# Inverse roots taken on ScalarE, squares summed on VectorE, and a first round that reaches into its third weight unit

## The reference, cut to what matters

```python
def _rmsnorm(x, g):
    y = x * rsqrt(mean(x * x, axis=-1) + 1e-6)
    return y * g

def _swiglu(h, w_in, w_out):
    gate, up = split(h @ w_in, 2)
    return (silu(gate) * up) @ w_out

for i in range(4):                       # g = norm_gains[i]
    h = h + 0.5 * _rmsnorm(_swiglu(_rmsnorm(h, g[0, 0]), ...), g[0, 1])
    h = h +       _rmsnorm(mixer(_rmsnorm(h, g[1, 0])),        g[1, 1])
    h = h + 0.5 * _rmsnorm(_swiglu(_rmsnorm(h, g[2, 0]), ...), g[2, 1])
```

## Time and profile before

| | us |
|---|---|
| three runs, median | 2501.04 |
| profiled execution, its own time | 2503.98 |
| its span | 2502.2 |
| PE busy | 2379.8 (95% of the span) |
| POOL busy | 1813.3 (72%) |
| DVE busy | 1481.2 (59%) |
| ACT busy | 1011.8 (40%) |
| granted TensorE clock, mean | 0.976 of 2.4 GHz |

### The profile page before, as it was taken

One profiled execution on the slowest core, in us unless ns is written; L12 is line 12 of the kernel. 1 busy time (PEld: TensorE's weight loads), 2 busy tenths in 40 slices (PEclk: granted clock), 3 DMA queues, 4 the chain that ended last, 5 costly groups with the idle time before them and its releaser, 6 DMA issues.

```text
span 2502.2 us, 53983 instructions
## 1 busy us (share of the span) xinstructions
PE 2379.8 (95%) x20898; PEld 2295.7 (92%) x20898; DVE 1481.2 (59%) x1830; ACT 1011.8 (40%) x1497; POOL 1813.3 (72%) x853
## 2 busy tenths in 40 slices
PE   6999999999999799999999788999999999999997
PEld 6999989999999789999999578988999999988997
DVE  5872137845862336863882868536882783234982
ACT  4344344344343434344443453324343434444342
POOL 5887827887887507886888696746888788746886
PEclk9999999999999989999999789999999999999999
DMA  5564614563564304563555132013555455433553
GB/s 168 175 195 129 180 61 135 171 206 118 170 194 127 119 19 141 168 200 119 173 183 170 70 113 83 4 37 95 175 183 169 143 178 192 135 109 101 174 188 109
DMA packets 89951, 348.87 MB, mean 139 GB/s; under 512 B 9968, under 2 KB 11760, under 8 KB 89712
## 3 DMA queue, kind: packets, MB, share of 16 engines
q1 hardware_dynamic: 89840, 347.31, 44.2%
HBM read 346.22 MB, written 1.05 MB: 139 GB/s over the span
## 4 chain that ended last, share of the span: by engine, by line
PE 83%; DVE 6%; POOL 4%; issue 3%; ACT 3%; DMA 0%; DVEq 0%; SPq 0%; ACTq 0%; POOLq 0%
PE bank L295 22%; PE bank L297 22%; PE bank L296 22%; PE bank L625 3%; POOL w_lo L1261 2%; PE bank L393 2%; PE bank L357 2%; PE bank L358 2%; PE bank L359 2%; PE bank L338 2%; POOL x_lo L1287 1%; DVE hid_hi L1475 1%; DVE hid L1473 1%; ACT w_hi L882 1%; PE bank L535 1%
## 5 line engine op out<-in xcount | busy, mean ns | idle before, releaser
L1261 POOL TENSOR_TENSOR w_lo<-raw,w_hi 128x1024 fp32r<-128x1024 f32 (+2 forms) x608 | 1604.1, 2663 | 594.6 <-ACT w_hi L882 572.3
L295 PE MATMUL bank<-x_hi,w_hi 128*128 128x272 f32 (+1 forms) x3380 | 991.7, 293 | 39.5 <-POOL x_lo L1287 16.3
L297 PE MATMUL bank<-x_hi,w_lo 128*128 128x272 f32 (+1 forms) x3380 | 981.8, 290 | 0.0
L296 PE MATMUL bank<-x_lo,w_hi 128*128 128x272 f32 (+1 forms) x3380 | 978.4, 289 | 0.0
L882 ACT ACTIVATE w_hi<-raw 128x1024 fp32r<-128x1024 f32 (+2 forms) x608 | 660.3, 1115 | 257.2 <-PE bank L297 204.5
L295 PEld LDWEIGHTS bank<-x_hi,w_hi 128*128 128x128 f32 x3380 | 643.6, 190 | 52.5 <-issue 30.4
L296 PEld LDWEIGHTS bank<-x_lo,w_hi 128*128 128x128 f32 x3380 | 645.3, 191 | 0.3
L297 PEld LDWEIGHTS bank<-x_hi,w_lo 128*128 128x128 f32 x3380 | 644.2, 191 | 0.0
L1477 DVE TENSOR_TENSOR hid_lo<-hid,hid_hi 128x272 f32 (+3 forms) x176 | 423.1, 2404 | 20.2
L295 PE MATMUL bank<-hid_hi,w_hi 128*128 128x272 f32 (+1 forms) x1408 | 404.9, 288 | 0.9 <-POOL w_lo L1261 0.8
L297 PE MATMUL bank<-hid_hi,w_lo 128*128 128x272 f32 (+1 forms) x1408 | 403.5, 287 | 0.0
(11 more groups left out here) (278 smaller groups left out, 2457.5 us busy)
## 6 DMA issues: line engine op xcount, KB each, us to landing
raw<-in_ffn_in SPq DMA_DIRECT2D x352, 512.0 KB, 3.6
raw<-in_ffn_out SPq DMA_DIRECT2D x128, 704.0 KB, 4.1
raw<-in_sb_in SPq DMA_DIRECT2D x48, 512.0 KB, 3.6
raw<-in_rw_in SPq DMA_DIRECT2D x24, 512.0 KB, 3.3
raw<-in_sb_out SPq DMA_DIRECT2D x16, 512.0 KB, 3.6
raw<-in_mla_out SPq DMA_DIRECT2D x8, 512.0 KB, 3.2
raw<-in_rw_lora SPq DMA_DIRECT2D x8, 512.0 KB, 4.7
raw<-in_rw_out SPq DMA_DIRECT2D x8, 512.0 KB, 3.2
```

What stands on the lines that cost most here:

```text
L295: nc.tensor.matmul(o, wh, xh[:, k, cols()], start=start, stop=False)
L296: nc.tensor.matmul(o, wh, xl[:, k, cols()], start=False, stop=False)
L297: last = nc.tensor.matmul(o, wl, xh[:, k, cols()], start=False, stop=stop)
L1261: nc.gpsimd.tensor_tensor(w_lo[:, s, w], raw[:, s, w], w_hi[:, s, w], ALU.subtract).then_inc(lo_ready, 1)
```

## The change

Three edits and what hangs on them.

1. The root and the reciprocal become a logarithm and an exponential on ACT, `exp(-0.5*ln(mean+eps))`, for every RMS norm, for `kk` and for the head norm. The result of the output norm is written straight to bank 4. Both functions are in one table set, which takes the place of the Sqrt table and of those loaded around the attentions; ACT has 21 table loads in place of 27. At the very first norm two loads are put in, one ahead of each of the two.
2. The squares of the eight tiles are added by DVE in three steps (4 tiles, 2, 1), and PE has one matmul by ones in place of eight. FILL goes from 25 to 17.
3. `first_round` runs units 0 and 1 with each tile and, where a norm stands ahead of it, a block of unit 2 with each odd tile; then the four blocks of unit 2 that are left, and all of unit 3. The sum stands behind the sixth of these twelve. In time mixing unit 2 comes whole and then unit 3.

```diff
-FILL = 25
+SUM_AFTER = 6
+FILL = 17
@@ PE
-            def input_sum(k, cut=None):
+            def input_sum(cut=None):
...
-                pe.wait_ge(hsq_ready, n["hsum"])
-                last = nc.tensor.matmul(bank[5][:, cut:L], ones, m[:, k, cut:L], start=k == 0, stop=k == DT_ - 1)
+                pe.wait_ge(hacc_ready, n["hsum"])
+                nc.tensor.matmul(bank[5][:, cut:L], ones, acc[:, cut:L], start=True, stop=True).then_inc(hsum_done, 1)
@@ first_round
+                paced, early = [], DT_ // 2 if behind_norm else 0
+                for k in range(DT_):
+                    paced += [(0, k), (1, k)] + ([(2, k // 2)] if early and k % 2 else [])
+                rest = [(2, k) for k in range(early, DT_)] + [(3, k) for k in range(DT_)]
+                for at, (s, k) in enumerate(paced + rest):
+                    if at == len(paced) + SUM_AFTER and behind_norm:
+                        input_sum(sum_cut)
+                    if k == 0:
+                        pe.wait_ge(lo_ready, sec.start + s + 1)
+                        pe.wait_ge(bank_free[s], uses[s] + 1)
+                    if s == 0:
+                        pe.wait_ge(x_ready, base + k + 1)
@@ latent attention
-                    if s == 0 and k or (s, k) in ((1, 6), (1, 7), (1, 0)):
-                        input_sum((k - 1) % DT_)
+                    if (s, k) == (3, 2):
+                        input_sum()
@@ ACT
-            def root(b, width, doubled=False):
-                nc.scalar.activation(std[:, cols()], bank[b][:, cols()], ACT.Sqrt, ...).then_inc(std_ready, 1)
+            def inverse_root(dst, b, width, doubled=False):
+                n["log"] += 1
+                nc.scalar.activation(std[:, cols()], bank[b][:, cols()], ACT.Ln, ...).then_inc(log_ready, 1)
+                act.wait_ge(log_ready, n["log"])
+                nc.scalar.activation(dst[:, cols()], std[:, cols()], ACT.Exp, scale=-0.5).then_inc(rstd_ready, 1)
...
-                nc.scalar.preload_act_table(ACT.Sqrt)
+                nc.scalar.preload_act_table_set("natural_log_exp_and_others")
...
                 def kk_roots():
-                    nc.scalar.preload_act_table(ACT.Sqrt)
                     act.wait_ge(kkmax_ready, 1)
-                    nc.scalar.activation(ex[:, :, :], ex[:, :, :], ACT.Sqrt, scale=64.0).then_inc(kkroot_ready, 1)
+                    nc.scalar.activation(ex[:, :, :], ex[:, :, :], ACT.Ln, scale=64.0).then_inc(kklog_ready, 1)
+                    act.wait_ge(kklog_ready, 1)
+                    nc.scalar.activation(ex[:, :, :], ex[:, :, :], ACT.Exp, scale=-0.5).then_inc(kkroot_ready, 1)
@@ DVE
             def input_norm():
-                inverse_root(xr)
+                n["hsq"] += DT_
+                dve.wait_ge(hsq_ready, n["hsq"])
+                steps.link(nc.vector.tensor_tensor(m[:, 0:4, cols()], m[:, 0:4, cols()], m[:, 4:8, cols()], ALU.add))
+                steps.link(nc.vector.tensor_tensor(m[:, 0:2, cols()], m[:, 0:2, cols()], m[:, 2:4, cols()], ALU.add))
+                nc.vector.tensor_tensor(acc[:, cols()], m[:, 0, cols()], m[:, 1, cols()], ALU.add).then_inc(hacc_ready, 1)
+                inverse_root()
...
-                steps.link(nc.vector.reciprocal(ex[:, :, :], ex[:, :, :]))
```

More of the change, by code:

```diff
@@ L346, in first_round @@
                 n["x"] += DT_
[L347 to L349 removed]
+                paced, early = [], DT_ // 2 if behind_norm else 0
[6 more added lines that the diff above has]
+                    if k == 0:
                         pe.wait_ge(lo_ready, sec.start + s + 1)
                         pe.wait_ge(bank_free[s], uses[s] + 1)
[L352 to L363 removed]
+                    if s == 0:
+                        pe.wait_ge(x_ready, base + k + 1)
+                    o, wh, wl = bank[s][:, cols()], w_hi[:, s, P * k:P * k + P], w_lo[:, s, P * k:P * k + P]
+                    nc.tensor.matmul(o, wh, x_hi[:, k, cols()], start=(k == 0), stop=False)
+                    nc.tensor.matmul(o, wh, x_lo[:, k, cols()], start=False, stop=False)
+                    last = nc.tensor.matmul(o, wl, x_hi[:, k, cols()], start=False, stop=(k == DT_ - 1))
+                    if k == DT_ - 1:
+                        last.then_inc(unit_used, 1)
             def whole(s, j):
@@ L871, in _ @@
         def _(act):
-            n = dict(sq=0, sg=0, norm=0, xf=0, h=0, hid=0, head=0, mhead=0, vt=0, hsum=0, kept=0, cut=0)
+            n = dict(sq=0, sg=0, norm=0, xf=0, h=0, hid=0, head=0, mhead=0, vt=0, hsum=0, log=0, kept=0, cut=0)
             cols = lambda: slice(n["cut"], L)
@@ L904, in finish_norm @@
                 act.wait_ge(sq_free, 2 + squares - n["kept"])
-                root(b, width)
+                inverse_root(rstd, b, width)
                 if not parts:
@@ L930, in gained @@
                     split_hi(secs[0], 0, 3, first=True)
-                    for k in range(DT_):
-                        nc.scalar.activation(m[:, k, cols()], h[:, k, cols()], ACT.Square).then_inc(hsq_ready, 1)
+                    nc.scalar.activation(m[:, :, cols()], h[:, :, cols()], ACT.Square).then_inc(hsq_ready, DT_)
             def input_root():
@@ L936, in input_root @@
                 act.wait_ge(hsum_done, n["hsum"])
-                root(5, D)
+                inverse_root(xr, 5, D)
             def norm_out(half):
@@ L942, in norm_out @@
                 n["kept"] += 1
-                root(4, D, half)
+                inverse_root(bank[4], 4, D, half)
             def squares_of(sec):
@@ L1071, in latent_attention @@
                 take_tiles(s_ukv, 4, lambda t: mk[:, t, :] if t < NH else mv[:, t - NH, :], every=1)
-                nc.scalar.preload_act_table(ACT.Exp)
                 take_values(mvt)
@@ L1215, in head_roots @@
                     act.wait_ge(var_done, 4 * half + 4)
-                    nc.scalar.activation(ystd[0:8, half, :], bank[4 * half][0:8, 0:L], ACT.Sqrt, bias=ln_eps_col[0:8, :]).then_inc(bank_free[4 * half], 1)
+                    nc.scalar.activation(ystd[0:8, half, :], bank[4 * half][0:8, 0:L], ACT.Ln, bias=ln_eps_col[0:8, :]).then_inc(bank_free[4 * half], 1)
+                    act.wait_ge(bank_free[4 * half], uses_at["ln"][4 * half] + 3)
+                    nc.scalar.activation(yrs[0:8, half, :], ystd[0:8, half, :], ACT.Exp, scale=-0.5).then_inc(yrs_ready, 1)
                 def high_part(k):
@@ L1394, in _, with inverse_root @@
             take = iter(secs)
-            def inverse_root(dst=rstd):
+            def inverse_root():
                 n["std"] += 1
-                dve.wait_ge(std_ready, n["std"])
-                steps.link(nc.vector.reciprocal(dst[:, cols()], std[:, cols()]))
+                dve.wait_ge(rstd_ready, n["std"])
             def low_part(layer, sub, k):
@@ L1448, in last_product @@
                 n["kept"] += 1
-                inverse_root(bank[4])
+                b = 2 if two else 3
+                dve.wait_ge(bank_free[b], uses_at[sec.name_key][b] + sec.iters + 1)
+                inverse_root()
                 for k in range(DT_):
@@ L1791, in head_norm @@
                     scaled(k)
-                inverse_roots(0)
                 for k in range(4, 8):
```

39 lines of the change are left out of this document (7 added, 32 removed).

## The result

Four runs of the changed kernel took 2463.29 to 2470.09 us, median 2467.36; four of the kernel before on the same chip 2500.37 to 2503.74, median 2500.72. The ratio is 0.9863, with a 95% interval from 0.9846 to 0.9880: faster by 33 us. The forecast was 2459, with a range from 2445 to 2481. The profiled execution took 2467.77 us itself, its span is 2466.0, its mean clock 0.977 (before 0.976).

The account below looks back on a forecast made before the run. PE's matmuls were 83% of the span, but a POOL-DVE-ACT loop set each SwiGLU's end. Terms 14.7+5.0+7.3+3.2+2.6+7.8+1.4=42.0 us off 2503.98 gave 2462.0, in medians 2459, range 2445 to 2481.

Parts of the forecast that it names:

- Output norm: At each boundary: reciprocal replaced by an exponential, factor ready 1.36 us earlier, only 0.47 us come through behind POOL's fourth split.
- First round: Round behind a boundary, X being the last `x_lo`'s end: ends at X+6.5, 3.65 us sooner; third addition starts X+2.0, split X+2.1.
- SwiGLUs and last norm: Seven SwiGLUs: root-to-POOL-run falls from 7.16 to 6.2 us, run starts 2.1 us sooner, 14.7 in all; last norm 1.4.
- The very first round: The eighth SwiGLU in-section, at the kernel's start: POOL's run starts at 36.3 against 41.3, gaining 5.0 us.
- Stick-breaking layers: Both PE-bound in their projections: 2x3.65=7.3 us, plus 0.94 twice for the table load ahead of the attention.
- rival A: At all ten boundaries but latent attention's, the third addition starts behind the split; about 11 us, 2470; chance 0.28.
- Latent attention: Entry gated by DVE moves 1.3 us earlier, reciprocals of `rstd` give 1.3; sum 2.6, plus 1.28 for the table load.
- Time mixing: Boundary 0.5 us, `rstd` 1.35, and 6 (bounds 2 to 10) for the reciprocal over `kk` leaving DVE; sum 7.8.
- B: SwiGLUs: the loop finds a shorter rhythm or was misjudged, PE's gain comes through; 7x1.6 us more, 2448; chance 0.10.
- C: `first_round`, ten times: with 8 fillers fewer PE idles and its clock falls; 6 us each, 2519; chance 0.03.
- D: At 26 norms Ln and Exp each need a table load: two of 1.28 us each, 67 us cost; given nothing.
- short waits for `w_lo` in every SwiGLU round: Sign of the forecast in PE, with POOL's runs of four still 12.17 us apart; under B there are none.

Follow-up runs that it names:

- e4: The kernel before with the first edit alone (logarithm and exponential for every root, with the table loads): 2489.35 us, ratio 0.9971.
- e2: As e1, with PE's sum of squares behind the third of the last twelve blocks in place of the sixth: 2464.61 us, ratio 0.9870.
- e6: As e5, with PE's sum of squares behind the third of the last twelve blocks: 2442.66 us, ratio 0.9783.
- e12: The kernel before, unchanged, in one more profiled execution: one run, 2498.68 us.
- e1: The changed kernel, but POOL waits for DVE's third addition before splitting the fifth unit, at every boundary with a sum: 2462.27 us, ratio 0.9863.
- e10: As e6, with filling matmuls (8, 2 and 5) in PE's three waits at the end of latent attention: 2443.02 us, ratio 0.9772.
- e11: The kernel before with nothing changed but `up` and `hid` in PSUM: 2491.05 us, ratio 0.9963.
- e8: As e1, but for `kk` DVE takes the reciprocal over 2176 columns again: 2460.88 us, ratio 0.9854.
- e7: The kernel before with the second edit alone (DVE's three additions, one sum on PE, FILL 17), `first_round` waiting for each weight unit by itself: 2491.99 us, ratio 0.9975.
- e3: As e1, with the third edit undone in the eight SwiGLUs and the two stick-breaking layers: 2462.23 us, ratio 0.9866.
- e9: As e6, with the third edit undone in the SwiGLUs and stick-breaking layers, the sum behind the fourth of sixteen blocks: 2451.49 us, ratio 0.9806.
- e5: As e1, with DVE writing `up` and `hid` in the SwiGLUs to spare banks of PSUM in place of SBUF: 2448.47 us, ratio 0.9810.

## Why the prediction was right, and where it was not

The forecast of 2459 was 8.4 us below the median, and the range held it. The sum was 5.8 us too large (42.0 against 36.2 between the two spans), and some of its reasons were wrong. Latent attention fell 6.3 short; the other differences nearly cancel.

- **Output norm**: right. The additions stand straight behind the fourth split, which is what let 0.47 us through; the pair on ACT took 0.91 where 0.97 was reckoned.
- **First round**: right in its times, X+2.00, X+2.13, X+4.39 and X+10.44 against X+2.0, 2.1, 4.3 and 10.5.
- **SwiGLUs and last norm**: 15.6 forecast (14.7 and 1.4, less the 0.5 counted with the very first round), 16.7 measured over seven sub-layers. The step that failed is "the reciprocal leaves ... 6.2 us", with "an earlier end needs an earlier first run of POOL" read as an earlier root. The root's chain is only one of two. In the kernel before, `hid` had taken 0.78 us, and I had booked 0.4 of it as a split that it would no longer meet, without asking when the splits themselves would end. e4 shows that the reciprocals alone give these sub-layers nothing, e2 that an earlier root gives none either, e6 that it does as soon as `hid` waits for no split. The gain of 2.2 is 1.7 from POOL's run, which starts 18.68 us behind the additions in place of 20.36, and 0.5 from the next output norm. The 1.7 stands because edit 1 moved one chain and edit 2 the other, to within 0.06 us of each other (15.37 and 15.31 behind the additions). The prediction had worked out only one of them, so that its number came true here was luck.
- **The very first round**: 5.5 forecast with the output norm behind it, 5.0 measured (5.4 against e12).
- **Stick-breaking layers**: about 9.2 for both with their table loads, 8.1 measured. In the second, rival A happened and took 1.1 (e1 gives 1.3 back). In the first, 1.3 of its 5.6 is where the lower clock fell in the one execution (e12); 4.3 is left of 4.6.
- **Latent attention**: 3.9 forecast, 2.5 lost. The entry's additions met two splits (I had worked out the race for units of eight blocks, and here they have six and come up sooner); the earlier `rstd` met POOL's run, which ate its 1.3; and PE stood at the lower clock for some 14 us at the end in place of 7, which cost up to 3.5. e10 shows the clock's share to hang on three waits of PE. The unchanged kernel took 155.5 in e12 and 157.8 in e11, and the versions with POOL's wait 155 to 158 (e10 aside), so that a gain of the size forecast is not shown here.
- **Time mixing**: 7.8 forecast, 8.9 measured; against the mean of the three unchanged executions it is 7.3. The place was right: the wait of 3.48 us in `v` with the lower clock behind it is gone, as the prediction had said, and PE reaches L625 some 3 us sooner. Its credit to the reciprocal over `kk` was not: put back into the changed kernel, it costs nothing (e8), and the waits unit by unit alone do as much as edit 1 alone (e7, e4). The rest of the gain is spread over the sub-layer, and which edit brings it stays open. e10, at 345.22 with nothing changed here against e6 (341.24), shows how far one execution can be off.
- **Rivals**: A came true at two boundaries of the changed kernel, one of them that of latent attention, which it had excepted, and at eight in e7. B, that PE's gain comes through in the SwiGLUs, is false for the changed kernel (e3) and true once DVE is freed (e9). C did not happen: the first boundary's round took X+6.5 as forecast, and the SwiGLUs' windows show 1.00. D did not happen: of the 21 table loads in the trace one stands between the two operations of a norm, at 29.91 in the very first, where it was put in. The sign "short waits for `w_lo` in every SwiGLU round" showed as two listed waits and, between them, delays of less than 0.1 us.

e6 beats both kernels, 0.9783 against the changed kernel's 0.9863; e10, at 0.9772, is not to be told from it by its total.

## What to carry to other kernels

Where two chains meet at one wait, work out both ends before crediting an edit to one; an edit that shows nothing alone may be half of a pair, and a short overlong operation (0.78 us for 0.44) is the sign that the other chain ends there. When a busy engine shares a resource, read its busy time by operation against the same operation elsewhere: DVE's was waiting for the most part, and two tensors moved to PSUM gave some 13 us, 20 with the sum three blocks earlier, beside the 34 of the change. A gain in a stretch with a varying clock needs a second execution of the kernel before, and an edit taken back tells its worth only beside the others that stand (e8).

## What the runs showed of the hardware

A DVE operation that reads two tensors of SBUF waits out a running POOL split, and the order of the two starts decides: 2.62 us for 0.44 where it started 0.05 behind, 0.44 where it was 0.13 ahead. What I had not expected is that a copy with a single tensor in SBUF (`hid_hi`) waits as well: it took 2.28 us beside splits of 1024 columns and up to 3.23 beside those of 1408, where it takes 0.30 by itself. Read from PSUM it took 0.42 to 0.44 each of its 176 times in e5, beside POOL's splits or not. Slower alone, it was faster by 0.75 in the mean. The Trainium skill (SBUF — State Buffer, "SBUF: two separate sides") names both kinds, operations with two inputs in SBUF and those in a two-port mode, to which it counts a float32 copy from SBUF to SBUF; the two durations agree with that.

PE's granted clock fell to 0.50 at the end of latent attention in each of the thirteen profiles without fillers there, and not with 15 filling matmuls in its three waits of 0.6 to 1.9 us (e10). How long it stayed low differed, from some 7 us in before to some 10 in e12, the same kernel, and some 14 in the changed one. At half the clock 7 us more cost up to 3.5, as much as a middle term of the prediction.
